# Other byte distances between the two operands of TensorE's matmuls, and squared ReLU in two tiles, in a two-layer hybrid trunk

## The reference

```python
for layer in range(DEPTH):                       # 2 layers
    h = rmsnorm(x, g[0])
    m = mixer_ab(h, ...) if layer % 2 == 0 else mixer_cd(h, ...)
    x = x + rmsnorm(m, g[1])
    h = rmsnorm(x, g[2])
    x = x + rmsnorm(cross_attn(h, mem, wq, wkv, wo), g[3])
    h = rmsnorm(x, g[4])
    x = x + rmsnorm(sq_relu_mlp(h, w1, w2), g[5])

def sq_relu_mlp(h, w1, w2):                      # 1024 -> 4096 -> 1024
    r = jax.nn.relu(h @ w1)
    return (r * r) @ w2
```

## The kernel before

| moving / stationary | start bytes (hi part) | distance | modulo 512 | modulo 256 |
|---|---|---|---|---|
| h / w | 90,688 / 16,512 | 74,176 | 448 | 192 |
| r / w | 157,696 / 16,512 | 141,184 | 384 | 128 |
| mem / w | 74,112 / 16,512 | 57,600 | 256 | 0 |
| mh / w | 183,168 / 16,512 | 166,656 | 256 | 0 |
| my / w | 141,248 / 16,512 | 124,736 | 320 | 64 |
| mp / w | 165,824 / 16,512 | 149,312 | 320 | 64 |
| k / q | 107,072 / 157,632 | -50,560 | 128 | 128 |
| pt / v | 182,656 / 141,248 | 41,408 | 448 | 192 |

## Time and profile before

### The profile page before, as it was taken

How to read it: one execution, slowest core, us unless ns; L and a number is a source line. 1 busy time by engine, 2 the same in 40 slices (tenths; PEclk the granted TensorE clock), 3 DMA queues, 4 the chain that set the end, 5 groups by cost and what they waited for, 6 DMA issues and landing times.

```text
span 978.5 us, 17155 instructions
## 1 busy us (share of the span) xinstructions
PE 910.6 (93%) x7268; PEld 882.9 (90%) x7268; DVE 666.1 (68%) x1013; ACT 471.7 (48%) x660; POOL 311.6 (32%) x213
## 2 busy tenths in 40 slices
PE   5978998999998999999989999999998799999997
PEld 5878987889898999999979988899998799999996
DVE  6797487777648655545588999986587285555553
ACT  4443443455546544444453432646465364444543
POOL 3232583643324100000058877546441330000000
PEclk8988998999999999999999999999999889999999
DMA  7442632455354565666545555335542435566661
GB/s 268 143 130 88 183 97 84 153 163 163 107 172 145 180 192 174 198 195 190 193 138 184 175 178 166 110 111 170 173 151 80 137 119 183 176 203 192 188 191 44
DMA packets 81031, 153.74 MB, mean 157 GB/s; under 512 B 6251, under 2 KB 7227, under 8 KB 80955
## 3 DMA queue, kind: packets, MB, share of 16 engines
q1 hardware_dynamic: 80843, 152.60, 49.6%
q10 hardware_dynamic: 112, 0.05, 0.0%
HBM read 151.58 MB, written 1.05 MB: 156 GB/s over the span
## 4 chain that ended last, share of the span: by engine, by line
PE 73%; DVE 15%; POOL 4%; ACT 4%; issue 3%; DMA 1%; DVEq 0%; POOLq 0%; ACTq 0%
PE ps L506 22%; PE ps L508 21%; PE ps L507 21%; POOL w_lo L1901 2%; DVE w_lo L1273 2%; DVE xc L1342 2%; PE ps L816 1%; ACT w_hi L929 1%; DVE xc L1339 1%; PE ps L745 1%; PE ps L747 1%; PE ps L746 1%; DVE ps L1628 1%; PE ps L573 1%; DVE E L1490 1%
## 5 line engine op out<-in xcount | busy, mean ns | idle before, releaser
L929 ACT ACTIVATE w_hi<-raw 128x1024 fp32r<-128x1024 f32 x284 | 296.7, 1056 | 272.4 <-DMA raw<-in_mlp_w 139.3
L506 PE MATMUL ps<-h_hi,w_hi 128*128 128x256 f32 x1280 | 365.2, 285 | 34.1 <-issue 12.8
L507 PE MATMUL ps<-h_lo,w_hi 128*128 128x256 f32 x1280 | 361.9, 283 | 0.0
L508 PE MATMUL ps<-h_hi,w_lo 128*128 128x256 f32 x1280 | 361.7, 283 | 0.0
L1273 DVE TENSOR_TENSOR w_lo<-raw,w_hi 128x1024 fp32r<-128x1024 f32 x192 | 251.5, 1329 | 138.7 <-ACT w_hi L929 138.4
L1901 POOL TENSOR_TENSOR w_lo<-raw,w_hi 128x1024 fp32r<-128x1024 f32 x92 | 229.1, 2505 | 185.3 <-ACT w_hi L929 185.3
L506 PEld LDWEIGHTS ps<-h_hi,w_hi 128*128 128x128 f32 x1280 | 248.5, 194 | 38.9 <-issue 16.5
L507 PEld LDWEIGHTS ps<-h_lo,w_hi 128*128 128x128 f32 x1280 | 248.2, 194 | 0.0
L508 PEld LDWEIGHTS ps<-h_hi,w_lo 128*128 128x128 f32 x1280 | 247.3, 193 | 0.0
L1924 POOL TENSOR_TENSOR rfac<-stat,mhalf 128x2 f32<-128x2 f32 (+1 forms) x14 | 16.6, 1183 | 419.9 <-DVE stat L1558 328.9
L508 PE MATMUL ps<-r_hi,w_lo 128*128 128x256 f32 x512 | 144.4, 282 | 0.0
(11 more groups left out here) (247 smaller groups left out, 1316.1 us busy)
## 6 DMA issues: line engine op xcount, KB each, us to landing
raw<-in_mlp_w SPq DMA_DIRECT2D x128, 512.0 KB, 3.9
raw<-in_cd_w_in SPq DMA_DIRECT2D x40, 512.0 KB, 3.7
raw<-in_xa_wkv SPq DMA_DIRECT2D x32, 512.0 KB, 4.0
raw<-in_ab_w_in SPq DMA_DIRECT2D x24, 512.0 KB, 3.8
raw<-in_xa_wq SPq DMA_DIRECT2D x16, 512.0 KB, 3.8
raw<-in_xa_wo SPq DMA_DIRECT2D x16, 512.0 KB, 3.9
raw<-in_cd_w_out SPq DMA_DIRECT2D x16, 512.0 KB, 3.9
raw<-in_ab_w_out SPq DMA_DIRECT2D x12, 512.0 KB, 3.8
```

The costliest lines, as they stand in the source:

```text
L506: nc.tensor.matmul(dst, wt[0], x[0], start=start, stop=False, skip_group_check=True)
L507: nc.tensor.matmul(dst, wt[0], x[1], start=False, stop=False, skip_group_check=True)
L508: return nc.tensor.matmul(dst, wt[1], x[0], start=False, stop=stop, skip_group_check=True)
L929: nc.scalar.activation(w_hi[:, v % SLOTS, :, :], raw[:, v % SLOTS, :, :], ACT.Copy)\
```

## The change

The gaps between tiles are changed, and `r_hi` and `r_lo` become two pairs of tiles, `r_even` and `r_odd`, one for each value of `h % 2`, with a gap between them. No instruction is added, removed or moved to another engine, and no wait changes.

```diff
         xT = sb("xT", [J, T])
-        skip(256)
+        skip(240)
         mem_hi, mem_lo = sb("mem_hi", [J, T], F32R), sb("mem_lo", [J, T], F32R)
-        skip(192)
+        skip(208)
         h_hi, h_lo = sb("h_hi", [J, T], F32R), sb("h_lo", [J, T], F32R)
...
         with ExitStack() as s:
+            skip(32, s)
             my_hi, my_lo = sb("my_hi", [J, T], F32R, s), sb("my_lo", [J, T], F32R, s)
...
             xdt = sb("xdt", [TT, D], scope=s)
+            skip(64, s)
             mp_hi, mp_lo = sb("mp_hi", [4, T], F32R, s), sb("mp_lo", [4, T], F32R, s)
...
         with ExitStack() as s:
+            skip(432, s)
             q_hi, q_lo = sb("q_hi", [J, T], F32R, s), sb("q_lo", [J, T], F32R, s)
             prob = sb("prob", [4, TT, T], scope=s)
-            skip(448, s)
+            skip(96, s)
             pt_hi, pt_lo = sb("pt_hi", [4, TT, T], F32R, s), sb("pt_lo", [4, TT, T], F32R, s)
         with ExitStack() as s:
-            skip(64, s)
-            r_hi, r_lo = sb("r_hi", [2, 4, T], F32R, s), sb("r_lo", [2, 4, T], F32R, s)
+            skip(112, s)
+            r_even_hi, r_even_lo = sb("r_even_hi", [4, T], F32R, s), sb("r_even_lo", [4, T], F32R, s)
+            skip(16, s)
+            r_odd_hi, r_odd_lo = sb("r_odd_hi", [4, T], F32R, s), sb("r_odd_lo", [4, T], F32R, s)
+            r_hi, r_lo = (r_even_hi, r_odd_hi), (r_even_lo, r_odd_lo)
...
-                                lambda kt: (r_hi[:, h % 2, kt, :], r_lo[:, h % 2, kt, :]),
+                                lambda kt: (r_hi[h % 2][:, kt, :], r_lo[h % 2][:, kt, :]),
```

More of the change, by code:

```diff
@@ L1119, in mlp @@
                         act.wait_ge(dve_made, after("dve", "rsq", l, i))
-                        nc.scalar.activation(r_hi[:, h % 2, 2 * q:2 * q + 2, :],
+                        nc.scalar.activation(r_hi[h % 2][:, 2 * q:2 * q + 2, :],
                                              rsq[:, q, :].rearrange("p (c t) -> p c t", c=2), ACT.Copy)\
@@ L1735, in low_r @@
                 dve.wait_ge(act_made, after("act", "r", l, h, q))
-                V.tensor_tensor(r_lo[:, h % 2, 2 * q:2 * q + 2, :], rsq[:, q, :].rearrange("p (c t) -> p c t", c=2),
-                                f(r_hi[:, h % 2, 2 * q:2 * q + 2, :]), ALU.subtract)\
+                V.tensor_tensor(r_lo[h % 2][:, 2 * q:2 * q + 2, :], rsq[:, q, :].rearrange("p (c t) -> p c t", c=2),
+                                f(r_hi[h % 2][:, 2 * q:2 * q + 2, :]), ALU.subtract)\
                     .then_inc(dve_made, tick("dve", "r", l, h, q))
```

## The result

The changed kernel takes 992.73 us (median of four runs, 990.23 to 995.05) against 985.42 for the kernel before in the same comparison (982.68 to 987.77). The ratio is 1.0093, 95% interval 1.0061 to 1.0125: slower by 0.9%. The quotient of the two medians is 1.0074. The forecast was 994.5 us. All ratios here are of executions in the chip's usual, fast state; two of the twelve of the experiment "Three more places" were slow and are left out of its ratio. The profiled execution took 990.23 us with a span of 988.5; the span before was 978.5. So what lies around a span is 1.7 us here, and most of the 6.5 us between the span and the median of before was spread between executions. The span of after is from the fastest of its four executions.

A forecast was written before the change was run, and what follows sets the result against it. PE's own matmul sequence was taken to bound the kernel. Terms of +0.4, +10.2, +0.2 and -0.2 us sum to +10.6; nine tenths, +9.5, on 985.0 gives 994.5 us, range 972 to 1,007.

The forecast's parts named there:

- What bounds the kernel: In the MLPs, PE's own matmul sequence was to set the speed, at 116.5 ns a matmul; outside them PE waits briefly.
- The places: Tile starts round to 32 bytes, so h moves 32 bytes, from 192 to 224 modulo 256 from its weights.
- The five pairs with a row: r_even, mh, my, mp and pt land on distances with already measured pitches; together +0.4 us.
- The three pairs without one: h, r_odd and k land between measured distances; the middle of the neighbours gave +10.2, +0.2 and -0.2 us.
- Nine tenths on the path: Of +10.6 us in PE's matmuls, nine tenths reach the end, +9.5 us, since slower pitch shortens waits for `w_lo`.
- The window count: The 163 us window in the first MLP stays full, with 1,379 matmuls in place of 1,401.
- h's pitch stays: Rival for h's matmuls: 32 bytes have no effect on their pitch; 985.4 us, chance 0.25.
- h at 120: Rival: h's matmuls go to the top level, 120.0 ns; 1,005 us, chance 0.25.
- the first case: h's pitch falls between the levels, at 115.5 to 118.5 ns; 988 to 1,001 us, chance 0.32.
- Faster places off multiples of 64: Rival: h, r_odd and k, starting in the middle of 64 bytes, go towards 111 ns; 971 us, chance 0.15.
- An odd start costs nothing in itself: Read from the convolution's taps, 216 ns each at half rate: starts at any multiple of 4 bytes add no cost.

The follow-up runs named there:

- Three more places: Kernel with all moving tiles at 192, except k/q at 128, pt/v at 64, first hidden block's squared ReLU at 32: 981.37 us, ratio 0.9957 to the kernel before.
- the gaps to the byte: The changed kernel with gaps exact to the byte, by views starting 16 bytes into a tile, h kept at 192: 986.66 us, ratio 1.0025 to the kernel before.

## Why the prediction was right

**What bounds the kernel.** That PE's own sequence sets the time held. PE's steps from start to start, where they are below 160 ns, add up to 771.7 us before and 785.7 after, +14.0. All other steps, the waits and the half-clock stretches among them, went from 195.6 to 191.5, -4.1. The sum is the +9.9 us by which PE's steps, and the span, grew. Not all of the 14.0 is pitch: 6,690 steps are below 160 ns after and 6,668 before, since less of that execution stood at half clock. Of the 7,267 steps, paired in order, 6,584 are below 160 ns at the full clock in both executions; these grew by 11.4 us, 13.0 of it h and the rest mostly r and mh getting shorter.

**The places.** They came out as worked out, byte for byte: h at 90,720, mem at 74,112, r split into 0 and 32. The change's stated aim, to leave h alone, was undone by the rounding to 32 bytes. With h put back the loss is gone (1.0004), and with h and k alone moved it is all there (1.0103). That h carries it is shown.

**The five pairs with a row.** mh 117.7, my 118.7, r_even 120.0 and mem 120.0 are the values taken from rows of tiles with that remainder, within 0.1 ns. mp went to a mean of 114.6, as forecast. pt at 64 had 116.6 in place of 117.7. Their forecast sum was +0.4 us; it didn't matter.

**The three pairs without one.** Here the middle between neighbours stood in for a value. h: 117.35 forecast, 118.3 measured, so the term is 3,840 x 3.6 = +13.8 us where +10.2 stood. r_odd: 118.85 forecast, 116.6 measured, -1.5 where +0.2 stood. k: 116.5 forecast, 118.2 measured, 0 where -0.2 stood. As a rule for a value in between, the middle isn't borne out: r_odd at 32 is below both of its neighbours. For h the error was 0.95 ns in 2.65.

**Nine tenths on the path.** The measured terms (h +13.8, r_even +1.0, r_odd -1.5, mh -0.8, my +0.2, mp -0.3, pt +0.1, k 0) add up to +12.5 us. Of these 9.9 us reached the span, eight tenths; by the medians it was 7.3 us. The share was near, but the reason given for it, that a slower pitch shortens PE's waits, isn't borne out: PE was idle 67.9 us before and 68.0 after. By the account of the steps, it was the clock that gave time back. At half clock stood 58.0 us of the span before and 48.6 us after, and the steps whose clock differs between the two executions took 2.0 us less after. This isn't a matter of the one execution profiled. The mean granted clock was 0.976 (0.971 to 0.982) in the 18 executions of the four kernels whose h is at 118.3 or 120.0, and 0.972 (0.965 to 0.980) in 88 of the kernel before that ran beside the experiments. By an estimate, 0.004 of 980 us is 4 us. Why more clock was granted there, no run shows. The forecast has no term for it. It was also luck that the errors cancelled: the terms were too small and the share too large, 10.6 x 0.9 = 9.5 where 12.5 x 0.8 = 9.9.

**The window count.** 1,379 matmuls were forecast and 1,379 counted. That is luck too: h is 0.95 ns higher and r's mean 1.1 ns lower than forecast, and in the MLP each moves in half of the matmuls.

**The rivals.** That h's pitch stays is refuted. h at 120 is refuted as a value, but 118.3 lies nearer to it than I thought and inside the first case only just. Faster places off multiples of 64: refuted by the gaps to the byte, where six such remainders gave 116.7 to 120. "An odd start costs nothing in itself", read from the taps at 216 ns, doesn't hold at the full rate: mh at 196, 4 bytes off a multiple of 16, was at 120.0 to 121.7. The rule of the Trainium skill, "TensorE: Matmul & The Clock Gate", Part 2, step 1, that two independent read ports keep a weight load from taking bandwidth from the running matmul, doesn't cover what the runs show: moving everything by 32 bytes does nothing, and moving h alone against the weights costs 1%. Why the distance acts, whether by a meeting of the two reads in one part of the memory or otherwise, no run shows.

## What to carry to other kernels

When matmuls run back to back, read their starts in the timeline by tile before looking for anything else: a pitch that differs between tiles of one form is time that a gap of some bytes can give or take. Work out where the allocator really puts a tile; here a rounding to 32 bytes turned a change of the other tiles into a move of the most used one. And a good distance alone isn't enough: at 192 the level was inherited in the MLPs from the work directly ahead, so a layout is judged by its sequence and on the chip, not tile by tile. When a gain or loss in the steps doesn't arrive whole, look at the granted clock before blaming the waits.

## What the hardware showed beyond that

- The pitch of a float32r matmul with 256 moving columns, at the full clock and with a new weight block each time, lay between 113.3 and 120.0 ns with both starts on multiples of 16, by the distance modulo 256: 0 had 120.0; 32, 116.7 or 117.8; 64, 117.8, and 113.3 in single stretches; 96, 120.0; 128, 118.7 or 120.0; 192, 113.3 or 117.8; 208, 119.2; 224, 118.3; 240, 117.3.
- 128 has a second level too: r came in on 120.0 behind an h at 117.8, and on 118.7 behind an h at 113.3, in both MLPs of the kernel before. So has 32: r_odd was at 116.7 behind h, and at 117.8 in the 96 matmuls directly behind an r_even at 120.0, in the changed kernel and in the one with h put back.
- In the kernels with h at 192, read from the starts: where r stood at 192 too, the h behind it without a pause kept r's level (20 of 20 on 113.3, 12 of 12 on 117.8), and behind an r at any other distance h came in on 113.3 (76 of 76). After a pause of PE, h at 192 was found on 113.3 in 135 stretches of 24 steps or more and on 117.8 in 78; what decides there is open.
- A moving operand that starts 4 bytes off a multiple of 16 stood at 120 to 121.7 ns at 196, and at 120 to 121 at 192 with the weights 4 bytes off as well.
- The kernels with the slower h were granted more clock: 0.976 in the mean of 18 executions, against 0.972 in 88 of the kernel before.
